# Two attention stages of a long kernel: fixed PSUM regions for scores and transposes, and gate products moved behind the transposes

## The reference, cut to what matters

```python
def gqa_attend(q, k, v, bias=None, sink=None):
    s = jnp.einsum("bqhgd,bkhd->bhgqk", q, k) * ATTN_SCALE
    if bias is not None:
        s = s + bias
    # with a sink: softmax over [s, sink], the sink's column dropped afterwards
    p = jax.nn.softmax(s, axis=-1)
    return jnp.einsum("bhgqk,bkhd->bqhgd", p, v)

# even layer: 8 heads "A" (all 512 + 256 keys), 8 heads "B" (band of 128 around the block, + 256 context
# keys, with a sink); context queries see the 256 context keys only
y = concat([oa * silu(ag), ob * silu(bg)]) @ w_out
# odd layer: a convolution branch oc, and 8 heads over 8 rows of a grid with a bias, + 256 context keys
y = concat([oc, od * silu(dg)]) @ w_out
```

## Time and profile before

| | |
|---|---|
| median of 3 runs | 2859.71 us (2857.09 to 2866.64) |
| the profiled execution's own time | 2864.18 us |
| its span | 2862.4 us |
| even attention stage | about 2129 to 2381 us of the span |
| odd attention stage | about 2652 to 2784 us of the span |
| PE busy over the span | 92% |

### The profile page before, as it was taken

One profiled execution on the slowest core, in us unless ns is written; L12 is line 12 of the kernel. 1 busy time (PEld: TensorE's weight loads), 2 busy tenths in 40 slices (PEclk: granted clock), 3 DMA queues, 4 the chain that ended last, 5 costly groups with the idle time before them and its releaser, 6 DMA issues.

```text
span 2862.4 us, 34696 instructions
## 1 busy us (share of the span) xinstructions
PE 2629.6 (92%) x13264; PEld 2107.0 (74%) x13264; DVE 1673.3 (58%) x3236; ACT 1134.4 (40%) x2071; POOL 0.2 (0%) x4
## 2 busy tenths in 40 slices
PE   7998899989999799898899899997989997899888
PEld 5876888668888578687876688886866666787556
DVE  6655565455446875565643644576376674398653
ACT  4235443433322332454444332323346673322562
POOL 0000000000000000000000000000000000000000
PEclk9989999989999899899999899996999998799898
DMA  4310033113226423101321232452110001122311
GB/s 146 99 52 16 2 118 111 43 65 98 96 98 220 139 81 99 38 1 45 120 87 57 69 96 96 161 192 92 52 37 16 23 16 33 34 81 67 69 43 45
DMA packets 73364, 218.33 MB, mean 76 GB/s; under 512 B 21232, under 2 KB 21488, under 8 KB 72560
## 3 DMA queue, kind: packets, MB, share of 16 engines
q1 hardware_dynamic: 48384, 176.29, 19.0%
q10 hardware_dynamic: 24816, 39.82, 4.4%
HBM read 213.98 MB, written 2.10 MB: 75 GB/s over the span
## 4 chain that ended last, share of the span: by engine, by line
PE 75%; DVE 13%; ACT 6%; issue 5%; DMA 1%; ACTq 1%; DVEq 0%; SPq 0%
PE bank L574 19%; PE bank L575 18%; PE bank L576 18%; PE bank L765 4%; PE bank L729 3%; DVE mod_part L2396 3%; PE bank L739 3%; ACT w_hi L533 2%; PE bank L1588 2%; PE bank L1183 1%; DVE w_lo L540 1%; PE bank L1191 1%; DVE hT L700 1%; PE bank L1129 1%; DVE y_x L693 1%
## 5 line engine op out<-in xcount | busy, mean ns | idle before, releaser
L574 PE MATMUL bank<-a_hi,w_hi 128*128 128x512 f32 (+1 forms) x1552 | 623.9, 402 | 43.5 <-ACT a_hi L603 21.7
L575 PE MATMUL bank<-a_lo,w_hi 128*128 128x512 f32 (+1 forms) x1552 | 613.1, 395 | 0.0
L576 PE MATMUL bank<-a_hi,w_lo 128*128 128x512 f32 (+1 forms) x1552 | 612.5, 395 | 0.0
L540 DVE TENSOR_TENSOR w_lo<-w_raw,w_hi 128x1024 fp32r<-128x1024 f32 x334 | 407.7, 1224 | 305.6 <-ACT w_hi L533 304.5
L533 ACT ACTIVATE w_hi<-w_raw 128x1024 fp32r<-128x1024 f32 x334 | 352.4, 1060 | 579.3 <-PE bank L576 486.5
L574 PEld LDWEIGHTS bank<-a_hi,w_hi 128*128 128x128 f32 (+1 forms) x1552 | 295.0, 190 | 132.6 <-issue 47.8
L576 PEld LDWEIGHTS bank<-a_hi,w_lo 128*128 128x128 f32 (+1 forms) x1552 | 295.1, 190 | 65.1
L575 PEld LDWEIGHTS bank<-a_lo,w_hi 128*128 128x128 f32 (+1 forms) x1552 | 295.2, 190 | 63.5 <-issue 3.0
L574 PE MATMUL bank<-b_hi,w_hi 128*128 128x512 f32 (+1 forms) x800 | 299.9, 375 | 36.0 <-DVE b_lo L713 23.5
L575 PE MATMUL bank<-b_lo,w_hi 128*128 128x512 f32 (+1 forms) x800 | 289.3, 362 | 0.0
L576 PE MATMUL bank<-b_hi,w_lo 128*128 128x512 f32 (+1 forms) x800 | 287.3, 359 | 0.0
(11 more groups left out here) (364 smaller groups left out, 3770.2 us busy)
## 6 DMA issues: line engine op xcount, KB each, us to landing
w_raw<-w_tiles SPq DMA_DIRECT2D x334, 512.0 KB, 3.4
mod_raw<-mod_tiles ACTq DMA_DIRECT2D x48, 512.0 KB, 3.5
d_bias<-rpb_rows ACTq DMA_DIRECT2D x16, 224.0 KB, 4.7
hT<-xT ACTq DMA_DIRECT2D x4, 512.0 KB, 11.2
m_in<-memT ACTq DMA_DIRECT2D x2, 1024.0 KB, 4.7
mod_cond<-cond_rows ACTq DMA_DIRECT2D x2, 1024.0 KB, 5.3
out<-hT ACTq DMA_DIRECT2D x8, 256.0 KB, 2.2
cT<-ctxT ACTq DMA_DIRECT2D x1, 1024.0 KB, 6.7
```

Source lines behind the costliest of these rows:

```text
L540: dve.tensor_tensor(w_lo[:, t % SPLIT, :], w_raw[:, t % RAW, :], w_hi[:, t % SPLIT, :].bitcast(f32), ALU.subtract).then_inc(sem("w_split"), 1)
L574: pe.matmul(o, wh, hi[:, k, :n], start=k == 0, stop=False)
L575: pe.matmul(o, wh, lo[:, k, :n], start=False, stop=False)
L576: mm = pe.matmul(o, wl, hi[:, k, :n], start=False, stop=k == kc - 1)
```

## The change: what it does

- PSUM becomes one tensor; `banks` are slices of it. `borrow` takes three neighbouring banks out of the rotation for a whole stage and `give_back` returns them with an event on which their next user waits. Banks 0 to 2 hold the scores of one pair, banks 3 to 5 the transposes of one pair. The rotation has the last two banks for everything else: gate products and values.
- In the three banks lane 0's columns end at column 768 and lane 1's begin there, its context part first, so that both units of a pair lie side by side. The pair's scores wait until DVE has read the pair before (`s_in` of its second unit), and the transposes of a pair wait until ACT has evicted the pair before (`pt_in`).
- DVE reads a unit without a mask in one instruction of up to 768 columns, and a masked unit in two that no longer depend on each other; the instruction that negates the maximum takes the larger of the two. ACT evicts the transposes of a pair in one or two instructions.
- PE's step is now: scores, values, transposes, filler. The filler of an even round is cut anew: all eight context blocks (256 columns) in the four latent steps, two in each, then all eight latent blocks (512 columns) in the two context steps, four in each. ACT evicts the context part at unit 8 of the round and the latent part at unit 0 of the next, and the weight splits move to units 9 (ACT) and 10 (DVE) of the next round. In the odd stage the gate's eviction and splits move by one to three units.

The core of the diff:

```diff
+        def wide_scores_pe(pe, key, us, units):
+            if us[0]:
+                v = us[0] - 1
+                pe.wait_ge(*when("s_in", *key, v, len(wide_maxima(units[v])) - 1))
+            order = [(us[0], 0), (us[1], 1), (us[1], 0), (us[0], 1)]
...
+                        if u == us[0] and i:
+                            pe.wait_ge(*when("bank_filled", "s", *key, us[1], i))
+                        pe.matmul(psum[:, 512 * SCORES + at:512 * SCORES + at + nk], q, k, start=True, stop=True)\
+                          .then_inc(*filled("s", *key, u, i))
...
+        def wide_turn_pe(pe, key, j, units, s):
+            if j:
+                pe.wait_ge(*when("pt_in", *key, j - 1))
+            for u in (2 * j, 2 * j + 1):
+                pe.wait_ge(*when("p", *key, u))
...
+            for i in range(n + ahead + 1):
+                if i < n:
+                    wide_scores_pe(pe, key, (2 * i, 2 * i + 1), units)
...
+                if pending is not None:
+                    us = group_of(units, pending)
+                    att_values_pe(pe, key, units, us, pt, vt, [("pt_in", *key, u // 2) for u in us[::2]])
+                    pending = None
+                if i == ahead:
+                    book.borrow(pe, TURNED, 3)
+                if 0 <= i - ahead < n:
+                    wide_turn_pe(pe, key, i - ahead, units, s)
+                    if group_end(units, 2 * (i - ahead) + 1):
+                        pending = 2 * (i - ahead) + 1
+                for _ in range(blocks(i)):
+                    next(fill, None)
...
+            for u in range(len(units) + 1):
+                if u < len(units):
+                    if before:
+                        before(u)
+                    maxima(u)
+                if u:
+                    divide(u - 1)
+                if between:
+                    between(u)
...
+            for u in range(2 * (n + ahead + 1)):
+                if u < len(units):
...
+                    act.activation(s[:, u % ns, :w], s[:, u % ns, :w], ACT.Exp, bias=att_col(u, 2),
+                                   accum_out=att_col(u, 3)).then_inc(*done("exp", *key, u))
+                between(u)
+                j = u // 2 - ahead
+                if u % 2 == 0 and 0 <= j < n:
+                    wide_evict_act(act, key, j, units, pt)
+                    if group_end(units, 2 * j + 1):
+                        pending.append((u + 3, 2 * j + 1))
+                if pending and pending[0][0] <= u:
+                    take(act, pending.pop(0)[1])
...
-            return 1 if i % (TT + MT) < TT else 2
+            return KC // TT if i % (TT + MT) < TT else KC // MT
...
             for name in E_GATE:
-                yield from product_steps(pe, (0,), both(name))
+                t = blocks[0] // KC
+                for p, src_hi, src_lo, n in reversed(both(name)):
+                    b = claim(pe, p, 0, hold=True)
...
+                            mm.then_inc(*(filled(p, 0) if n == M else book.tile_used(p, 0)))
+                            book.release(p, 0)
...
+            c, rest = divmod(u, 2 * (TT + MT))
+            if rest == 2 * TT and c < KC:
+                even_gate_evict_act(act, c, PARTS[1])
+            if rest == 0 and 1 <= c <= KC:
+                even_gate_evict_act(act, c - 1, PARTS[0])
+            if (rest == 2 * TT + 1 and 1 <= c < KC) or (rest == 1 and c == KC):
+                hi_after(act, f"{E_GATE[c - 1]}/lat", 0)
```

More of the change, by code:

```diff
@@ L325, in claim @@
         self.jobs[key] = n, self.uses[n]
+        if n in self.lent:
+            pe.wait_ge(*self.when(*self.lent.pop(n)))
         if self.uses[n]:
@@ L331, in claim, with borrow, give_back @@
         return banks[n]
+    def borrow(self, pe, first, count):
+        for n in range(first, first + count):
+            assert n not in self.held, n
+            self.held.add(n)
+            if n in self.lent:
+                pe.wait_ge(*self.when(*self.lent.pop(n)))
+            if self.uses[n]:
+                pe.wait_ge(self.sem(f"bank_free{n}"), self.uses[n])
+    def give_back(self, first, count, *event):
+        for n in range(first, first + count):
+            self.held.discard(n)
+            self.lent[n] = event
     def release(self, *key):
@@ L887, in attention_act, with wide_parts, wide_first, wide_slots @@
                         pending = v
+        SCORES, TURNED, HALF = 0, 3, S + M
+        def wide_parts(unit):
+            return list(enumerate(unit["parts"]))[::1 if unit["lane"] == 0 else -1]
+        def wide_first(unit, turned):
+            lane, parts = unit["lane"], unit["parts"]
+            if len(parts) == 1 and not turned:
+                return (0, 2 * S)[lane]
+            return HALF - sum(nk for _, nk, _, _ in parts) if lane == 0 else HALF
+        def wide_slots(unit):
+            kts = [kt for _, (k0, nk, _, _) in wide_parts(unit) for kt in range(k0 // P, (k0 + nk) // P)]
+            return [wide_slot(unit["lane"], kt) for kt in kts]
@@ new lines, in wide_slot, with wide_tiles, wide_maxima @@
+        def wide_slot(lane, kt):
+            return kt if lane == 0 else TT + MT + (kt - TT if kt >= TT else kt + MT)
+        def wide_tiles(buffer):
+            slots = buffer[:, :, :, :].rearrange("p l k q -> p (l k) q")
+            return lambda lane, k0, k1, q0, q1: slots[:, wide_slot(lane, k0):wide_slot(lane, k0) + 1, q0:q1]
+        def wide_maxima(unit):
+            parts = wide_parts(unit)
+            if all(mask is None for _, (_, _, _, mask) in parts):
+                return [(0, sum(nk for _, (_, nk, _, _) in parts), None, [i for i, _ in parts])]
+            out, c = [], 0
+            for i, (_, nk, _, mask) in parts:
+                out.append((c, nk, mask, [i]))
+                c += nk
+            return out
@@ new lines, in wide_act @@
+        def wide_act(act, key, units, s, buffer, take, between):
+            ns = s.shape[1]
+            n, ahead = len(units) // 2, ns // 2 - 1
+            pt = buffer[:, :, :, :].rearrange("p l k q -> p (l k) q")
+            pending = []
+            for u in range(2 * (n + ahead + 1)):
+                if u < len(units):
+                    w = sum(nk for _, nk, _, _ in units[u]["parts"])
+                    act.wait_ge(*when("max", *key, u))
+                    if units[u]["sink"] is not None:
+                        act.activation(att_col(u, 5), units[u]["sink"], ACT.Exp, bias=att_col(u, 2))\
+                           .then_inc(*done("exp_sink", *key, u))
+                    act.activation(s[:, u % ns, :w], s[:, u % ns, :w], ACT.Exp, bias=att_col(u, 2),
[8 more added lines that the diff above has]
+                    take(act, pending.pop(0)[1])
+            assert not pending, pending
```

151 lines of the change are left out of this document (117 added, 34 removed).

## The result

The changed kernel takes 2890.91 us (median of 4 runs, 2888.16 to 2895.52) against 2860.31 of the kernel before beside it: ratio 1.0106, 95% interval 1.0084 to 1.0128. Timed a second time it came to 1.0121 (1.0102 to 1.0140). It is slower, as forecast, but by 30 to 35 us instead of 16, above the whole range.

A forecast was written before the change was run, and what follows sets the result against it. PE's queue was taken to bound the kernel; A rounds +5.2, B rounds +9.2, first round +0.5, end -2.4, odd stage -1 and clock +4.5 gave +16 us on a 2859.7 median: 2876, range 2849 to 2888.

The forecast's parts named there:

- The wait inside a pair: Scores: unit one's last part before unit two's context part; nothing at 512 columns, about 0.3 us a round at 256.
- the trip: From one latent pair's scores through DVE's two reads to the next pair's scores: 4.52 us, setting the short steps.
- A round: Even stage, six pairs with A heads: 31.65 us against 31.86 before, plus a 1.95 us wait for a bank.
- The clock: PE's clock falls to the 1.2 GHz level behind three of seven waits: +4.5 us, bounds 0 and 10.
- B rounds: Even stage, rounds of six pairs with B heads: 29.0 us against 28.65, plus a 1.95 us wait for a bank.
- Rival 3: PE's clock falls in every wait and in some short steps: 11.5 + 15 us, 2886; chance 0.10.
- The values' bank: In each round's fifth step values wait for ACT's gate eviction: 1.95 us, seven rounds, 13.6 us.
- Rival 2: The values never meet the gate's bank, by another alternation of banks: no clock loss, 2857 us; chance 0.25.
- Rival 1: DVE's reads return by 3.6 us instead of 4.52 and do not set the short steps: 2847 us; chance 0.18.
- PE's own work: PE's instructions alone, with fewer array shape changes at about 0.08 us each: 29.06 us a round with A heads.
- First round: First round of the even stage, where no values wait for the gate's bank: +0.5 us.
- Odd stage: Second pair's scores wait for DVE's bias, +1.9 us; bias loads' delay absorbed, -2.6; with smaller terms -1 in sum.

The follow-up runs named there:

- e2_hold: Changed kernel with the gate's context bank given back one step later in the plan; ratio 1.0057 to the kernel before, 16 us faster than the changed kernel.
- e1_order: Changed kernel with lane 1's context part issued ahead of lane 0's latent part; ratio 1.0083 to the kernel before, 8.7 us faster than the changed kernel.
- the probe: Changed kernel where lane 1's first part also waits for lane 1's context part; ratio 1.0196 to the kernel before, 24 us slower than the changed kernel.

## Why the prediction was right or wrong

**The step that failed** is "The wait inside a pair ... costs nothing at 512 columns, where the lane is busy until then". It costs 0.36 in every such pair, because the completion of lane 1's short part is told only behind lane 0's long one. That lifts PE's own steps and the trip alike: an A round without bank waits is 33.37 us (e2_hold), forecast 31.65. Three A rounds are +5.2. Of the 1.72 a round the order of the parts takes back 1.35; with it changed the steps are 5.53, 4.58, 4.68, 4.58, where I had 5.53, 4.52, 4.66, 4.52. Another 0.23 lies in t4, 7.81 where I had 7.58, since the values wait until 0.84 for the transposes' eviction. Over the whole kernel the wait inside the pair cost 8.7 us by e1_order.

**The clock** was the second term that was mis-sized. I had three of seven waits fall, +4.5. Five fell, with a stretch in t2 at 2200 us besides: 237.85 less 100.1 (three A rounds of 33.37), 114.6 (the four B rounds; both from e2_hold) and 14.0 of waits leaves 9.2 us. Rival 3 had the mechanism, but at "every wait" it was wrong too: behind the last two waits the clock did not fall. That its 2886 lies nearer to the measured time than my 2876 is luck, since it too had nothing for the pair's wait. The Trainium skill (TensorE: Matmul & The Clock Gate, A second HAM failure mode) tells of a kernel in which short idles between groups of matmuls, while it cycles through PSUM, swing the clock between its two levels. The trace agrees: 0.95 over the stage with the waits, 0.98 without.

**The values' bank**: right in place, cause, number and size: seven waits, 14.0 us of idle PE against 13.6. Rival 2 is out.

**The trip**: right that it sets t1 and t3, and DVE's part to 0.01 us; its total was 0.38 short through the pair's wait. Rival 1 is out: for it DVE had to be back so early that the trip no longer sets the short steps, and it set them in A rounds at 4.90 and in B rounds at 4.15 and 3.87, each time with PE waiting for DVE. The 3.87 is below the 4.0 that I had named as its sign, but I had 4.1 for that step.

**B rounds**: I took 29.0 against 28.65. Without bank waits they are 28.36, the first 29.48: -0.9 for four instead of +1.4. t1 to t3 are 4.15, 4.39 and 3.87 where I had estimated 4.5, 4.5 and 4.1 from masked reads.

**PE's own work** and the cheaper changes of array shape: right once the pair's wait is gone (t0 is 5.53 in e1_order).

**First round** +3.9 instead of +0.5 (+5.2 in the second pair of profiles): the pairs' wait again, and a pair at half clock at 2128.64 (row of 3.39 instead of 1.92). With the order changed it is 2.1 us shorter in the trace (27.6 against 29.7); the rest was not tested by itself. **End of the even stage** -2.5 against -2.4: right.

**Odd stage**: forecast -1, measured +3.6 by time and +6 to +7 by traces. The start's wait was within its bounds; the first transposes' wait of 2.3, whose cause is read from the code and not tested, and the pair's wait (4.5) were missing.

Together: forecast +16. A +5.2, clock +4.7, first round +3.4, odd stage +4.6 to +8, B and the rest -2 make 32 to 35, against 30 to 35 measured. The range failed because the cost that I had set at nothing and the one that I had taken as three of seven were errors of the same sign, with the odd stage's missing waits beside them, and the range was drawn from the rivals alone.

## What to carry to other kernels

Where two lanes of the array share a chain of matmuls, let a wait point only to work issued ahead of everything long: moving one short part to the front of its pair gave 8.7 us and no wait was removed. When a fixed region takes banks out of a rotation, write down every claim of a round against every eviction; with two banks left, giving one back a step later in the plan was worth 16 us. Price an idle of 2 us on a saturated PE at more than itself: here 14 us of waits cost about 22 by the trace of the stage, and 16 by the timing with some 4 of uncertainty on either side; and expect part of any gain ahead of a wait to reappear in that wait.

## What the runs showed of the hardware that I had not expected

- PE tells of its completions in the order of issue, across both lanes: the first two counts of a 512-column pair come 1.14 and 1.18 us after its start with the short part issued second, 0.71 and 1.14 with it issued first. A matmul that waits for the short part starts 0.10 us behind the long one's end (0.49 us of idle weight loads in the changed kernel, 0.92 in the probe). The ends of matmuls are modelled in these rows; the starts and counts are recorded.
- Between the two lanes even the starts are not in the order of issue: 2700.60 for lane 1's second matmul, 2700.81 for lane 0's second, issued ahead of it.
- After idles of about 1.9 us behind 0.7 us of work the granted clock fell to its 1.2 GHz level five times in seven, in both profiles of the changed kernel; t4 without the idle kept 1.00 (e2_hold). Which of the seven fall I can't derive.
- Ahead of the even stage one and the same program differed by 11.6 us between two profiles, while a stage of 228 us repeated within 0.1.
